# Short merge jobs of a hybrid attention block moved forward and spread by running sums

## The chip, the cores and the metric

The kernel runs on one core of one Trainium2 chip. The metric is the device time of one execution in microseconds (us). Five engines work side by side and meet only at semaphores: TensorE (PE), ScalarE (ACT), VectorE (DVE), GpSimd (POOL) and SyncE (SP), which here only issues transfers.

## What is computed

The input x has 256 tokens of 2048 channels. In short:

```
h  = RMSNorm(x);  z = h @ w_in            # q, k, v, gate of 16 heads, forget logits, two merge gates
oa = rmsnorm(diff_attention(...)) * silu(ga);   ya = oa @ w_proj_a      # 8 heads
ob = forgetting_attention(...)    * silu(gb);   yb = ob @ w_proj_b      # 8 heads
m  = sigmoid(ma) * ya + sigmoid(mb) * yb
out = RMSNorm(x + m @ w_out)
```

All is float32. Each product is made of three TensorE passes over operands split into a high and a low half (hi*hi, hi*lo, lo*hi).

## The kernel before

**Jobs.** The weights come in tiles of 128 x 1024 floats (512 KB). A job is one such tile. It is loaded by SyncE into one of four raw slots (`load`, L291 on); ScalarE makes its high half (`split`, L614), VectorE its low half (`split`, L845), each in a ring of four slots; TensorE multiplies it (`tile` and `sum_tile`, matmuls on L342 to L344). Job t + 4 may be split only when TensorE has done job t, since it takes the ring slot. All engines go through the jobs in one fixed order; in the iteration of job t ScalarE splits job t + 4, and VectorE splits job t + 4 and, where that job needs it, adds for job t + 5.

**Long jobs.** Chunk c (2 to 15) is the input projection of head c: eight long jobs of 12 matmuls, 512 columns each, into two PSUM banks (one for each half of the tokens). When the last is done, ScalarE empties both banks into `z_sb` (`evacuate`, L619); TensorE may write these banks again only after that (`banks_free`). The projections of the forgetting branch (FOX, 16 jobs), of the differential branch (DIFF, 16 jobs) and the output projection (OUT, 32 jobs) are long jobs too. The code numbers the chunks from 0; the jobs of chunk 2 begin at job 20.

**Short jobs.** The merge gates are computed by a Strassen-like scheme: for each of four groups seven products P1, P5, P6, P3, P7, P4, P2 in this order, each of four short jobs of 6 matmuls, 112 in all. They write bank Z2 or Z3 in turn. For P5, P6, P7 and P4 VectorE first combines the raw weights with an earlier tile (`add`, L858 and L860, 128 x 1024). P1 and P5 are copied out by ScalarE (`keep`), the others are added by VectorE (`fold`, L869 to L881: P6 and P7 take two additions of 128 x 512, the others one). The sums of activations that P5, P6, P3 and P7 need are split in four parts (ScalarE L682, VectorE L968) at the jobs in `PARTS_AT`.

**Order.** Each of the chunks 3 to 15 and the first half of FOX has 16 jobs, 8 long and 8 short, nearly alternating (`HEAD_STEPS`, `SUM_STEPS`); a chunk ends with a long job and two short ones, and begins with a long one. Chunk c's long jobs use banks Z0 and Z1 (chunk 2: Z2 and Z3). Chunks 2, DIFF, OUT and the second half of FOX hold long jobs alone.

**Attention.** The attention of head b is done beside the jobs, in two bursts on TensorE after a given job: X (`X_AT`: transposes of the gated output of b - 2, of the probabilities of b - 1, of q and k of b) and Y (`Y_AT`: values of b - 1, scores of b). Around them ScalarE does copies, exponentials and tanh, VectorE the low half of q and k (L986), the gate (L991), the gated output (L1021) and the masked maxima (L979, L981), GpSimd the bias of the next forgetting head (L1207, L1212) or the rotary embedding. `O_SPLIT_AT` places the splits of attention outputs.

The wait of a short job for its bank is, in `sum_tile`:

```python
fill = FORMS * g + f
if fill < 2:
    pe.wait_ge(evac[0], 4)      # chunk 2 evacuated
    pe.wait_ge(evac[1], 4)
else:
    form_taken(fill - 2)
```

Of the kernel before, what the change touches and what calls it, by code (L numbers as in the profile page):

```python
# [44 lines left out]
HEAD_STEPS, SUM_STEPS = (0, 2, 4, 6, 8, 10, 12, 13), (1, 3, 5, 7, 9, 11, 14, 15)  # L45
FOX_STEPS, FOX_SUM_STEPS = (0, 2, 4, 5, 8, 11, 14, 15), (1, 3, 6, 7, 9, 10, 12, 13)
SUM_JOB = ([MIXED_JOB + 16 * c + u for c in range(N_HEADS - 3) for u in SUM_STEPS] + [FOX_JOB + u for u in FOX_SUM_STEPS])
SUM_OF = {job: s for s, job in enumerate(SUM_JOB)}
X_AT = {21: 0, 28: 1, 38: 2, **{MIXED_JOB + 16 * (b - 2) + 4: b for b in range(3, N_HEADS)},
        FOX2_JOB + 1: N_HEADS, DIFF_JOB + 1: N_HEADS + 1}  # L50
Y_AT = {25: 0, 33: 1, 43: 2, **{MIXED_JOB + 16 * (b - 2) + 9: b for b in range(3, N_HEADS)}, FOX2_JOB + 5: N_HEADS}
# [10 lines left out]
def head_job(c, j):  # L62
    if c == 0:
        return j
    return PLAIN_JOB + j if c == 2 else MIXED_JOB + 16 * (c - 3) + HEAD_STEPS[j]


# [16 lines left out]
DIFF_OF = {diff_job(n, j): (n, j) for n in range(4) for j in range(4)}  # L84

# [18 lines left out]
def build(nc, x, xT, xg, consts_in, w_main, w_fl, g_final, out):  # L104
# [11 lines left out]
    with ctx:  # L116
# [6 lines left out]
        def sem(name):  # L123
# [89 lines left out]
        LAST = ((0, slice(3 * CHUNK, 4 * CHUNK), Z[0]),  # L213
                (1, slice(3 * CHUNK, 7 * CHUNK // 2), Z[1]), (1, slice(7 * CHUNK // 2, 4 * CHUNK), A))
# [125 lines left out]
        def _(pe):  # L340
# [197 lines left out]
            for job in range(MIXED_JOB, FOX_JOB):  # L538
                if job in HEAD_OF:
                    c, j = HEAD_OF[job]  # L540
                    if j == 0:
                        banks_free(4 if c == 3 else fill_of(c) + 1)
                    z_tile(c, j)
                else:
                    sum_tile(SUM_OF[job])
                attention(job)

            def fox_tile(n, j):
                if j == 0:
                    banks_free((18, 19, 19, 20)[n])  # L550
                    if n == 2:
                        form_taken(FORMS * GROUPS - 2)
                        form_taken(FORMS * GROUPS - 1)
                if n == 0:
                    pe.wait_ge(o_split, j // 2 + 1)
                tile(fox_job(n, j), 1 if n == 2 else 0, oT_hi, oT_lo, 2 * j, 2, CHUNK, j == 0, j == 3)

            for job in range(FOX_JOB, DIFF_JOB):
                if job in FOX_OF:
                    fox_tile(*FOX_OF[job])  # L560
                else:
                    sum_tile(SUM_OF[job])
# [40 lines left out]
        def _(act):  # L603
# [223 lines left out]
        def _(dve):  # L827
# [238 lines left out]
            def fox_gate(n):  # L1066
# [3 lines left out]
                for m in range(M_TILES):  # L1070
                    dve.scalar_tensor_tensor(m_all[:, n, m, :], gates[:, n, m, 1, :], 1.0, Z[(2 if n == 2 else 0) + m][:],
                                             ALU.add, ALU.mult).then_inc(evac[m], 1)

            def diff_gate(n):
# [5 lines left out]
                for m in range(M_TILES):  # L1080
                    dve.scalar_tensor_tensor(m_b[:, m, :], gates[:, n, m, 0, :], 1.0, Z[2 * (1 - n % 2) + m][:],
# [224 lines left out]
```

## Time and profile before

| | us |
|---|---|
| median of 3 runs (740.04 to 740.54) | 740.09 |
| the profiled execution | 740.02 |
| its span, first to last instruction | 738.2 |
| TensorE busy | 728.4 |
| VectorE busy | 560.0 |
| ScalarE busy | 438.3 |
| GpSimd busy | 84.2 |

An engine's busy time counts its instructions' durations; matmuls overlap, so starts tell more than durations. In a timeline a row has the start, the time taken (of the merged instructions), engine, line, operation, output and inputs, the count, and in brackets the idle time before it and what ended it. By the trace chunk 3 begins at 77.9 us, each mixed chunk takes about 35 us, FOX begins at 537.2 and DIFF at 595.6.

### The profile page before, as it was taken

To read this page: it belongs to the slowest core of one execution; us is meant where nothing else is said; L and a number is where in the kernel's file an instruction comes from. 1 tells how busy PE (TensorE), PEld (TensorE's weight loads), DVE (VectorE), ACT (ScalarE), POOL (GpSimd) and SP (SyncE) were. 2 spreads that over 40 slices of the span, in tenths; PEclk is the share of its full clock that TensorE was granted. 3 is DMA by queue.
4 is the path that set the end of the run, shared out by engine and by line. 5 is a ranking of instruction groups with operands and counts; after the bars stand their busy time and mean duration, and the time that the engine had idled before them with its cause. 6 is when DMAs were issued, how large, how long until landed. Compare 5 with 4: busy or idle time off the path is not lost.

```text
span 738.2 us, 9729 instructions
## 1 busy us (share of the span) xinstructions
PE 728.4 (99%) x3538; PEld 609.4 (83%) x3538; DVE 560.0 (76%) x724; ACT 438.3 (59%) x652; POOL 84.2 (11%) x105
## 2 busy tenths in 40 slices
PE   8999999999999999999999999999999999999996
PEld 6998888888888888888888888888888888888886
DVE  6775798779669778877978976988998657655552
ACT  7963667466656565666656667667567544444531
POOL 0000223103010201010302010202020000001110
PEclk9999999999999999999999999999999999999999
DMA  8668465776956676785586766566677656756632
GB/s 330 212 209 332 146 228 203 250 225 236 340 171 237 220 248 224 271 289 192 203 273 199 270 247 262 198 259 224 221 249 248 200 193 228 292 191 187 193 140 115
DMA packets 47230, 168.97 MB, mean 229 GB/s; under 512 B 5256, under 2 KB 5264, under 8 KB 46672
## 3 DMA queue, kind: packets, MB, share of 16 engines
q1 hardware_dynamic: 46064, 164.97, 64.6%
q10 hardware_dynamic: 864, 1.84, 0.7%
q0 software_dynamic: 256, 1.54, 0.5%
q8 instruction: 29, 0.48, 0.3%
q14 instruction: 17, 0.14, 0.1%
HBM read 166.23 MB, written 2.11 MB: 228 GB/s over the span
## 4 chain that ended last, share of the span: by engine, by line
PE 94%; DVE 2%; issue 2%; DMA 1%; ACT 1%; SPq 0%; DVEq 0%; POOLq 0%; POOL 0%; ACTq 0%
PE Z L342 29%; PE Z L343 28%; PE Z L344 28%; PE Z L503 3%; PE A L444 1%; DVE w_lo L845 1%; PE A L410 1%; DMA w_raw<-in_w_main 1%; PE B L426 1%; PE Dk L435 1%; PE B L423 1%; DVE gates L912 1%; PE C L453 0%; ACT w_hi L614 0%; PE A L461 0%
## 5 line engine op out<-in xcount | busy, mean ns | idle before, releaser
L845 DVE TENSOR_TENSOR w_lo<-w_raw,w_hi 128x1024 fp32r<-128x1024 f32 (+1 forms) x240 | 290.5, 1215 | 113.4 <-ACT w_hi L614 110.9
L614 ACT ACTIVATE w_hi<-w_raw 128x1024 fp32r<-128x1024 f32 (+1 forms) x235 | 243.7, 1044 | 184.5 <-PE Z L344 162.3
L342 PE MATMUL Z<-w_hi,hT_hi 128*128 128x512 f32 (+2 forms) x720 | 274.4, 381 | 0.5 <-DVE w_lo L845 0.5
L344 PE MATMUL Z<-w_hi,hT_lo 128*128 128x512 f32 (+2 forms) x720 | 272.7, 379 | 0.0
L343 PE MATMUL Z<-w_lo,hT_hi 128*128 128x512 f32 (+2 forms) x720 | 272.7, 379 | 0.0
L342 PEld LDWEIGHTS Z<-w_hi,hT_hi 128*128 128x128 f32 x720 | 135.3, 188 | 26.9 <-issue 0.6
L344 PEld LDWEIGHTS Z<-w_hi,hT_lo 128*128 128x128 f32 x720 | 135.3, 188 | 25.4
L343 PEld LDWEIGHTS Z<-w_lo,hT_hi 128*128 128x128 f32 x720 | 135.3, 188 | 24.5
L342 PE MATMUL Z<-w_hi,sum_hi 128*128 128x512 f32 x256 | 101.2, 395 | 0.0
L344 PE MATMUL Z<-w_hi,sum_lo 128*128 128x512 f32 x256 | 99.8, 390 | 0.0
L343 PE MATMUL Z<-w_lo,sum_hi 128*128 128x512 f32 x256 | 99.7, 390 | 0.0
L845 DVE TENSOR_TENSOR w_lo<-x_and_g,w_hi 128x1024 fp32r<-128x1024 f32 x64 | 80.3, 1255 | 25.1 <-ACT w_hi L614 24.2
L614 ACT ACTIVATE w_hi<-x_and_g 128x1024 fp32r<-128x1024 f32 x64 | 67.9, 1060 | 52.1 <-DVE x_and_g L860 32.6
L860 DVE TENSOR_TENSOR x_and_g<-w_raw,x_and_g 128x1024 f32<-128x1024 f32 x48 | 59.1, 1232 | 2.7 <-DMA w_raw<-in_w_main 2.7
L344 PEld LDWEIGHTS Z<-w_hi,sum_lo 128*128 128x128 f32 x256 | 48.1, 188 | 10.2
L342 PEld LDWEIGHTS Z<-w_hi,sum_hi 128*128 128x128 f32 x256 | 48.1, 188 | 9.7 <-issue 0.3
L343 PEld LDWEIGHTS Z<-w_lo,sum_hi 128*128 128x128 f32 x256 | 48.1, 188 | 9.5
L1207 POOL TENSOR_TENSOR bias<-gates,c_nat 128x128 f32<-128x128 f32 (+1 forms) x16 | 16.3, 1040 | 151.3 <-DVE neg_max L981 145.6
L619 ACT ACTIVATE z_sb<-Z,rstd 128x512 f32<-128x512 f32 x29 | 18.4, 686 | 20.9 <-PE Z L344 19.8
L1237 POOL TENSOR_TENSOR o_rstd<-o_ms,neg_half 128x2 f32<-128x2 f32 x8 | 9.2, 1156 | 188.1 <-DVE o_ms L1058 188.1
L1225 POOL TENSOR_TENSOR rope_t<-z_sb,consts 128x64 f32<-128x64 f32 x32 | 14.7, 492 | 111.1 <-ACT z_sb L619 111.1
L858 DVE TENSOR_TENSOR w_raw<-x_and_g,w_raw 128x1024 f32<-128x1024 f32 x16 | 19.7, 1229 | 5.0 <-DMA w_raw<-in_w_main 5.0
(184 smaller groups left out, 567.4 us busy)
## 6 DMA issues: line engine op xcount, KB each, us to landing
w_raw<-in_w_main SPq DMA_DIRECT2D x283, 512.0 KB, 4.1
x_and_g<-in_w_main SPq DMA_DIRECT2D x16, 512.0 KB, 7.1
w_raw<-in_w_fl SPq DMA_DIRECT2D x8, 264.0 KB, 3.0
o_T<-in_x SPq DMA_DIRECT2D x1, 2048.0 KB, 7.9
x_and_g<-in_xT SPq DMA_DIRECT2D x4, 256.0 KB, 5.9
gates<-c_rows_dram POOLq DMA_DIRECT2D x1, 1024.0 KB, 6.1
z_sb<-in_g_final SPq DMA_DIRECT2D x1, 1024.0 KB, 9.9
x_and_g<-in_xT ACTq DMA_DIRECT2D x3, 256.0 KB, 7.3
```

Of the source, the lines that this page charges most:

```text
L342: pe.matmul(acc, a_hi, b_hi, start=first, stop=False)
L343: pe.matmul(acc, a_hi, b_lo, start=False, stop=False)
L344: return pe.matmul(acc, a_lo, b_hi, start=False, stop=last)
L503: mm = pe.matmul(Z[m][:], x_part[:, 2 * j + kk, m * P:(m + 1) * P], w_part[:, kk], start=(j == 0 and part == 0 and kk == 0), stop=(j == TI ...
L614: act.activation(w_hi[:, t % RING, 0:cols_of(t)], weights(t), ACT.Copy).then_inc(hi_ready, 1)
L619: act.activation(z_sb[:, c % Z_SLOTS, m], Z[(2 if c == 2 else 0) + m][:], ACT.Copy, scale=rstd[:, m:m + 1]).then_inc(evac[m], 1)
L845: dve.tensor_tensor(w_lo[:, t % RING, 0:n], weights(t), w_hi[:, t % RING, 0:n].bitcast(fp32), ALU.subtract).then_inc(lo_ready, 1)
L858: dve.tensor_tensor(raw, chain[:, q, :], raw, ALU.subtract).then_inc(added, 1)
L860: dve.tensor_tensor(chain[:, q, :], raw, chain[:, q, :], ALU.subtract).then_inc(added, 1)
L1207: pool.tensor_tensor(bias[:, sl].unsqueeze(1), rows.rearrange("p (h n) -> p h n", h=HEADS)[:, h:h + 1, 0:n], c_nat[:, m, h:h + 1].unsqueez ...
L1225: ins = pool.tensor_tensor(rope_t[:, i], u, v, ALU.mult)
L1237: pool.tensor_tensor(o_rstd[:], o_ms[:], neg_half[:], ALU.pow).then_inc(o_rstd_ready, 1)
```

## The change

All 112 short jobs now stand in chunks 3 to 12, 7 to 16 in each (`SUMS_IN`). `ORDER` writes out each chunk as a string of `h` (long) and `s` (short). Chunks 13, 14, 15 and FOX have long jobs only. Bursts and splits get new places. Long jobs of a chunk without short ones, and everything behind, take the two pairs of banks in turn (`PAIR`). Chunk 3 now begins with three short jobs, at job 28. The total count of jobs, DIFF and OUT stay as they are.

```diff
-HEAD_STEPS, SUM_STEPS = (0, 2, 4, 6, 8, 10, 12, 13), (1, 3, 5, 7, 9, 11, 14, 15)
-FOX_STEPS, FOX_SUM_STEPS = (0, 2, 4, 5, 8, 11, 14, 15), (1, 3, 6, 7, 9, 10, 12, 13)
+SUMS_IN = {3: 11, 4: 11, 5: 15, 6: 10, 7: 16, 8: 10, 9: 9, 10: 13, 11: 10, 12: 7, 13: 0, 14: 0, 15: 0, 2: 0}
+ORDER = {3: 'ssshssshshshshshshh', 4: 'ssshssshshshhshshsh', 5: 'shhssshssshssshssshshsh', 6: 'shshhssshssshshshh', 7: 'shshshshssshssshssshsssh', 8: 'shshshshhssshsshsh', 9: 'shshhshshshshsssh', 10: 'ssshssshssshshshshshh', 11: 'ssshsshshshshhshsh', 12: 'shshhssshsshhhh', 13: 'hhhhhhhh', 14: 'hhhhhhhh', 15: 'hhhhhhhh', 2: 'hhhhhhhh'}
+CHUNK_JOB = [0, 0, PLAIN_JOB]
+for c in range(3, N_HEADS + 1):
+    CHUNK_JOB.append(CHUNK_JOB[-1] + len(ORDER[c - 1]))
+BURST_X = {3: 8, 4: 8, 5: 3, 6: 4, 7: 4, 8: 4, 9: 4, 10: 8, 11: 7, 12: 4, 13: 2, 14: 2, 15: 2}
+BURST_Y = {3: 13, 4: 12, 5: 14, 6: 12, 7: 11, 8: 8, 9: 8, 10: 15, 11: 12, 12: 11, 13: 6, 14: 6, 15: 6}
-O_SPLIT_AT = {FOX_JOB - 20: 0, FOX_JOB - 14: 1, FOX2_JOB + 3: 2, FOX2_JOB + 4: 3}
+O_SPLIT_AT = {CHUNK_JOB[14] + 1: 0, CHUNK_JOB[14] + 4: 1, CHUNK_JOB[15] + 4: 2, FOX_JOB + 7: 3}
+PAIR = [0, 1, 0, 1]
+for c in range(3, N_HEADS):
+    PAIR.append(0 if SUMS_IN[c] else 1 - PAIR[-1])
+for n in range(11):
+    PAIR.append(1 - PAIR[-1])
-            def banks_free(fill):
-                pe.wait_ge(evac[0], fill - 1)
-                pe.wait_ge(evac[1], fill - 1)
+            def banks_free(fill, pair):
+                before = [n for n in range(fill) if PAIR[n] == pair]
+                if before:
+                    pe.wait_ge(evac[0], before[-1] + 1)
+                    pe.wait_ge(evac[1], before[-1] + 1)
```

The first jobs of the chunks are 28 (chunk 3), 47, 66, 89, 107, 131, 149, 166, 187, 205 (chunk 12), 220, 228 and 236 (chunk 15); FOX begins at 244 and DIFF, as before, at 260. In the new order P1 takes jobs 28, 29, 30, 32, P5 33, 34, 36, 38, P6 40, 42, 44, 47, P3 48, 49, 51, 52 and P7 53, 55, 57, 60. The first X bursts follow jobs 21, 28, 40 and 55, the Y bursts jobs 25, 32, 45 and 59.

## Rows read from the trace of the kernel before

**Rows 1.** The page: busy time of the engines; granted clock in 40 slices

```profile
PE 728.4 (99%) x3538; PEld 609.4 (83%) x3538; DVE 560.0 (76%) x724; ACT 438.3 (59%) x652; POOL 84.2 (11%) x105
...
PEclk9999999999999999999999999999999999999999
```

**Rows 2.** Timeline of PE: first matmul of job 28; around short job 58

```profile
77.90 0.39 PE L342 MATMUL Z<-w_hi,hT_hi 128*128 128x512 f32 x1
...
146.86 0.39 PE L344 MATMUL Z<-w_hi,hT_lo 128*128 128x512 f32 x1
...
148.45 0.39 PE L342 MATMUL Z<-w_hi,sum_hi 128*128 128x512 f32 x1
```

**Rows 3.** Timelines of DVE and PE around the one gap

```profile
296.56 1.21 DVE L845 TENSOR_TENSOR w_lo<-w_raw,w_hi 128x1024 fp32r<-128x1024 f32 x1
...
297.45 0.39 PE L344 MATMUL Z<-w_hi,hT_lo 128*128 128x512 f32 x1
297.92 0.47 PE L342 MATMUL Z<-w_hi,hT_hi 128*128 128x512 f32 x1
```

**Rows 4.** Groups of DVE by line and shape: busy us, mean ns

```profile
L845 DVE TENSOR_TENSOR w_lo<-w_raw,w_hi 128x1024 fp32r<-128x1024 f32 x232 | 284.9, 1233 | 109.9 <-ACT w_hi L614 107.4 <-ACT w_hi L814 1.8
...
L986 DVE TENSOR_TENSOR qkT_lo<-A,qkT_hi 128x384 fp32r<-128x384 f32 x16 | 8.8, 552 | 0.7 <-ACT qkT_hi L688 0.7
...
L991 DVE SCALAR_TENSOR_TENSOR gate<-gate_tanh,z_sb 128x256 f32<-128x256 f32 x16 | 6.7, 419 | 0.0
...
L869 DVE TENSOR_TENSOR gates<-Z,gates 128x512 f32<-128x512 f32 x4 | 2.7, 682 | 0.0
```

**Rows 5.** Timeline of DVE: a Y burst's work, adds, low halves

```profile
118.38 0.60 DVE L1021 SCALAR_TENSOR_TENSOR og<-A,inv,gate 128x128 f32<-128x128 f32 x2
...
119.45 1.22 DVE L860 TENSOR_TENSOR x_and_g<-w_raw,x_and_g 128x1024 f32<-128x1024 f32 x1
120.59 1.42 DVE L845 TENSOR_TENSOR w_lo<-w_raw,w_hi 128x1024 fp32r<-128x1024 f32 x1
121.94 1.63 DVE L845 TENSOR_TENSOR w_lo<-x_and_g,w_hi 128x1024 fp32r<-128x1024 f32 x1
...
123.56 1.41 DVE L860 TENSOR_TENSOR x_and_g<-w_raw,x_and_g 128x1024 f32<-128x1024 f32 x1
```

**Rows 6.** Timeline of ACT: the evacuations of chunks 2 and 4

```profile
78.10 1.27 ACT L619 ACTIVATE z_sb<-Z,rstd 128x512 f32<-128x512 f32 x2
79.26 1.06 ACT L614 ACTIVATE w_hi<-x_and_g 128x1024 fp32r<-128x1024 f32 x1
80.20 1.06 ACT L682 ACTIVATE sum_hi<-gates 128x1024 fp32r<-128x1024 f32 x1
...
147.29 1.27 ACT L619 ACTIVATE z_sb<-Z,rstd 128x512 f32<-128x512 f32 x2 [1.66 <-PE Z L344]
```

**Rows 7.** Waits of DVE from 77.9 to 537.2: total, times, longest

```profile
DVE w_lo L845 <- ACT w_hi L614: 68.8, 75, 2.6
DVE w_raw L858 <- DMA w_raw<-in_w_main: 5.0, 7, 2.1
```

**Rows 8.** Timeline of PE: before and after an X burst, a Y burst

```profile
80.39 0.40 PE L344 MATMUL Z<-w_hi,hT_lo 128*128 128x512 f32 x1
...
81.31 0.48 PE L342 MATMUL Z<-w_hi,hT_hi 128*128 128x512 f32 x1
...
171.03 0.39 PE L344 MATMUL Z<-w_hi,hT_lo 128*128 128x512 f32 x1
...
172.50 0.39 PE L342 MATMUL Z<-w_hi,hT_hi 128*128 128x512 f32 x1
```

**Rows 9.** Timeline of POOL: the bias of one head

```profile
119.61 2.87 POOL L1207 TENSOR_TENSOR bias<-gates,c_nat 128x128 f32<-128x128 f32 x2 [19.46 <-DVE neg_max L981]
122.56 2.73 POOL L1212 TENSOR_TENSOR bias<-bias,consts 128x128 f32<-128x128 f32 x2
```

**Rows 10.** Transfers by tile: count, KB each, median us to landing

```profile
w_raw<-in_w_main SPq DMA_DIRECT2D x283, 512.0 KB, 4.1
```

More of the change, by code:

```diff
@@ L59, in fill_of, with max_count @@
     return c if c < 2 else c + 1
+def max_count(heads):
+    return 2 * heads + 2 * max(0, heads - HEADS)
 def head_job(c, j):
@@ L64, in head_job @@
         return j
-    return PLAIN_JOB + j if c == 2 else MIXED_JOB + 16 * (c - 3) + HEAD_STEPS[j]
-def max_count(heads):
-    return 2 * heads + 2 * max(0, heads - HEADS)
+    return CHUNK_JOB[c] + [u for u, kind in enumerate(ORDER[c]) if kind == "h"][j]
 def fox_job(n, j):
-    return FOX_JOB + FOX_STEPS[4 * n + j] if n < 2 else FOX2_JOB + 4 * (n - 2) + j
+    return FOX_JOB + 4 * n + j
 def diff_job(n, j):
@@ L355, in tile @@
                 mm.then_inc(w_used, 1)
-            def banks_free(fill):
-                pe.wait_ge(evac[0], fill - 1)
-                pe.wait_ge(evac[1], fill - 1)
+            def banks_free(fill, pair):
[3 more added lines that the diff above has]
+                    pe.wait_ge(evac[1], before[-1] + 1)
+                if pair == 1 and fill > FIRST_SUM_FILL:
+                    form_taken(FORMS * GROUPS - 2)
+                    form_taken(FORMS * GROUPS - 1)
             def z_tile(c, j):
-                tile(head_job(c, j), 1 if c == 2 else 0, hT_hi, hT_lo, 2 * j, 2, CHUNK, j == 0, j == TILES - 1)
+                tile(head_job(c, j), PAIR[fill_of(c)], hT_hi, hT_lo, 2 * j, 2, CHUNK, j == 0, j == TILES - 1)
             def form_taken(fill):
@@ L549, in fox_tile @@
                 if j == 0:
[L550 to L553, printed above, removed]
+                    banks_free(FOX_FILL + n, PAIR[FOX_FILL + n])
                 if n == 0:
                     pe.wait_ge(o_split, j // 2 + 1)
-                tile(fox_job(n, j), 1 if n == 2 else 0, oT_hi, oT_lo, 2 * j, 2, CHUNK, j == 0, j == 3)
+                tile(fox_job(n, j), PAIR[FOX_FILL + n], oT_hi, oT_lo, 2 * j, 2, CHUNK, j == 0, j == 3)
             for job in range(FOX_JOB, DIFF_JOB):
[L559 to L562, printed above, removed]
+                fox_tile(*FOX_OF[job])
                 attention(job)
             for n in range(4):
-                banks_free(21 + n)
+                banks_free(DIFF_FILL + n, PAIR[DIFF_FILL + n])
                 for j in range(4):
@@ L576, in _ @@
             for n in range(3):
-                banks_free(25 + n)
+                banks_free(OUT_FILL + n, PAIR[OUT_FILL + n])
                 for j in range(TILES):
@@ L618, in evacuate @@
                 for m in range(M_TILES if c >= 2 else 1):
-                    act.activation(z_sb[:, c % Z_SLOTS, m], Z[(2 if c == 2 else 0) + m][:], ACT.Copy,
+                    act.activation(z_sb[:, c % Z_SLOTS, m], Z[2 * PAIR[fill_of(c)] + m][:], ACT.Copy,
                                    scale=rstd[:, m:m + 1]).then_inc(evac[m], 1)
@@ L1126, in residual @@
                 sl = slice(n * CHUNK, (n + 1) * CHUNK)
-                dve.tensor_tensor(y_sb[:, m, sl], Z[2 * (1 - n % 2) + m][:], x_res[:, m, sl], ALU.add).then_inc(evac[m], 1)
+                dve.tensor_tensor(y_sb[:, m, sl], Z[2 * PAIR[OUT_FILL + n] + m][:], x_res[:, m, sl], ALU.add).then_inc(evac[m], 1)
             for n in range(3):
```

36 lines of the change are left out of this document (19 added, 17 removed).

## The prediction

> **What bounds the kernel now.** I read the page's busy shares first, then who waited for whom, then TensorE's timeline. TensorE is busy 728.4 of 738.2 us at the full granted clock [rows 1]. Busy alone says little for a pipelined engine, so I went by starts: the last matmul of long job 57 starts at 146.86, and the six of short job 58 and one more later it is 148.45 [rows 2]: 1.59 / 7 = 0.227 us from start to start of 512-column matmuls. A long job (12 matmuls) is 2.72 us, a short one (6) is 1.36 us. From chunk 3 on TensorE stands still behind a low half once: VectorE ends at 297.77, TensorE starts at 297.92, where 297.68 was due, so 0.25 us is lost and 0.14 us passes from an end to the start that it releases [rows 3]. TensorE's own work is the bound, VectorE is just fast enough, and nothing but those 0.25 us is there to be won in the stages that the change touches.
>
> **The change, part by part.** It removes no matmul, add, fold or transfer. It moves 112 short jobs from thirteen chunks and the FOX stage into chunks 3 to 12, and leaves chunks 13 to 15 and FOX with long jobs alone.
>
> *VectorE's prices.* A low half lasts 1.23 us, an add the same [rows 4, 5], and starts follow each other at 1.14 us [rows 5], as ops overlap by 0.09; a high half on ScalarE takes 1.06 and its starts are 0.95 apart [rows 6]. A short job with an add thus asks 2.28 us of VectorE for 1.36 us of TensorE; a long job asks 1.14 for 2.72. The low half of job t+4 can't begin before TensorE is through job t, for its ring slot and the high half. So VectorE leads by three jobs at most: 6.8 us with alternating jobs, 4.1 to 5.4 where short jobs stand together. On average VectorE would do (it waits 68.8 us for ScalarE in 77.9 to 537.2 [rows 7]), but slack before a clump can't be stored beyond three jobs. I walked the clumps.
>
> *(a) Job 28, the first after chunk 2.* Before it is a long job in banks Z0 and Z1, so TensorE goes on at 77.90 while ScalarE empties Z2 and Z3 from 78.10 to 79.37 [rows 2, 6]. Now job 28 is a short job that writes Z2, and its first matmul waits for both evacuations: 79.37 + 0.14 - 77.90 = **1.6 us**. Behind it every later matmul is late; nothing covers it.
>
> *(b) Six chunk boundaries.* At the starts of chunks 5 to 9 and 12 (by the code's numbers) only one short job stands between the last long job of the chunk before and the first of the new one, in the same banks. Take the evacuation of chunk 4: its last long matmul starts at 146.86, a short job would end at 148.45, ScalarE's two evacuations end at 147.29 + 1.27 = 148.56 [rows 2, 6], plus 0.14: 0.25 us. Six times 1.5; at two of the six (8 and 12) ScalarE first waits for an add ahead of the evacuation, at an estimated 0.4 each. **2.3 us.** Before, two short jobs stand there and hide it.
>
> *(c) Chunk 3, jobs 28 to 37.* Time from the end of job 27. TensorE: job 28 ends at 1.6 + 1.36 = 3.0; then the X burst 0.69 and the Y burst 1.24 [rows 8], short jobs 29, 30, 32, 33, 34, 36 (8.2) and long 31, 35 (5.4): job 37 is due at 18.5. VectorE: ScalarE evacuates first, so the high half of 31 ends at 2.4; low half 31, sum_lo part, add 33 bring VectorE to 5.8. Then low halves 32 to 37, adds 34, 36, 38 and a sum_lo part, 10 x 1.14 = 11.4, and the head's own work: qkT_lo 0.55 and gate 0.42, less the overlaps 0.8 [rows 4], og and maxima 1.07, from 118.38 to 119.45 [rows 5]: 19.1, usable at 19.3. Late by 0.8. While GpSimd adds a head's bias, VectorE's ops last 1.42, 1.63 and 1.41 us in place of 1.23, 0.8 us in all [rows 5, 9]; with it 1.6. I take **1.3 us**.
>
> *(d) Chunk 4, jobs 47 to 54.* Time from the end of long job 46. TensorE: 47, 48, 49 short, 50 long: 51 is due at 6.8. ScalarE evacuates (0.2 to 1.35), makes high half 50 (to 2.4), sum_hi (to 3.4), high half 51 (to 4.3). VectorE: low half 50 to 3.6, sum_lo to 4.75, the two chained adds of the P6 fold (0.68 each [rows 4]) to 6.2, low half 51 to 7.4: ready 7.57, late 0.76. Add 53 and low half 52 follow: ready 9.85 where 8.93 was due, late 0.92. Then low half 53, add 55, low half 54: ready 13.34 where 12.57 was due, late 0.77. **2.45 us.** Before, long jobs alternate there.
>
> *(e) The other clumps* (jobs 76 to 86, 95 to 101, 123 to 130, 171 to 179, 188 to 193) have a similar mix, but no evacuation, sum split and fold together at their start. Three marginal delays of 0.3: **0.9 us**, an estimate between 0 and 3. The bounds come from (c) and (d): none if VectorE enters with a full lead, one more chunk 4 if not.
>
> *(f) Transfers.* A raw load takes 4.1 us from issue to landing [rows 10] and VectorE already waits seven times, 5.0 us, for loads of P7 [rows 7]. In a clump a slot's next load has three jobs of VectorE, 3 x 2.28 = 6.8 us, to land, so I cost it at nothing. Where VectorE catches up through P3 or P2 jobs the cover is only three short jobs, 4.1 us; losing it costs under 1 us a place, 2 to 3 us in all.
>
> *(g) Chunks 13 to 15 and FOX.* Long jobs alone, VectorE leads by up to three long jobs; banks alternate, so evacuations are covered by a whole chunk. Probabilities of a head are combined three jobs after its Y burst, and the next X burst comes at the fourth: some 2 us of cover. Nothing gained, as TensorE lost nothing there before; nothing lost. If the cover is gone, a few tenths four times. The O splits move within chunks in which both engines idle: nothing. The pair chosen for the out stage only swaps banks.
>
> Minus the 0.25 us of now: 1.6 + 2.3 + 1.3 + 2.45 + 0.9 - 0.25 = **+8.3 us**. The profiled execution took 740.02 us (span 738.2), the median is 740.09; both give 748.3.
>
> **A rule weighed against the trace.** While GpSimd works, VectorE's ops stretched to between 1.41 and 1.63 us [rows 5], not to the length of GpSimd's two pairs of 2.87 and 2.73 us [rows 9]. The Trainium skill (SBUF — State Buffer, "Who interferes with whom") says that a VectorE op with two SBUF inputs and a GpSimd op that reads SBUF exclude each other, and that the later one blocks for the other's whole instruction. By that rule the sum would go up as in rival 3; the rows here show a smaller price.
>
> **The rivals.**
> 1. *Low halves keep up; only banks wait.* The planner's running sum may place shorts where VectorE has its idle time, and my walks chain durations without slack. Then (a) and the six plain waits stay: 1.6 + 1.5 - 0.25, **742.9**. For it: 68.8 us of slack [rows 7]. Against: 2.28 against 1.36 us. Chance 0.17.
> 2. *More clumps late, and loads with them.* (e) at its upper end (+2) and (f) at 3: **753**. For it: loads are waited for even now. Chance 0.14.
> 3. *GpSimd's bias blocks VectorE fully* in the clumps: 5.6 us of GpSimd per head [rows 9] less the 0.8 counted would cost up to 4.8 more in each of (c) and (d), of which I count 3 each: **754.3**. Against: rows 5. Chance 0.05.
> 4. *Not slower.* ScalarE's evacuation is wholly behind the single short job, every low half is in time and the gap of rows 3 goes: 740.1 + 1.6 - 0.25 = **741.4**, inside what can't be told from no change. It decides at job 51: if its low half is ready 6.8 us after job 46, this case or rival 1 holds. If job 28's wait too were partly hidden, the time would be just under before. Chance 0.08. That the change doesn't do what it says I see no way for: the order is written out.
>
> **How the numbers follow.** My forecast (746 to 751.5) has 0.56. The range 742.5 to 753.5 leaves out rivals 3 and 4 and half of what lies at rival 2's upper end, about 0.2. About 0.2%, 1.5 us, is what a measurement of this kernel can tell from no change. Slower by more than that: the forecast and rivals 1 to 3, 0.92; within: most of rival 4, 0.05; faster: its rest, 0.03.
>
> **What would show it.** TensorE should idle about 1.6 us before job 28, released by ScalarE's z_sb; about 0.25 us at six chunk starts, released the same way; and 0.7 to 1 us three times between jobs 51 and 54, released by VectorE's low half. VectorE's waits for ScalarE should move from chunks 3 to 12 to chunks 13 to FOX. TensorE's 0.227 us should not move. The prediction is wrong if the low halves of 51 to 54 are in time, if the bursts of chunks 13 to 15 wait, or if waits behind loads are a main item.

## The result, and the profile after

The changed kernel is slower: median 754.91 us of 6 executions (751.96 to 756.27) against 740.07 us (739.71 to 740.54) before; ratio 1.0193, 95% interval 1.0177 to 1.0208. That is +14.8 us where +8.3 was forecast, and above the range. Two things stand out. The profiled execution is the fastest of the six (751.96 us, span 750.1), and the executions lie 4.3 us apart, where those of before lie within 0.8. So 11.9 us can be read in the trace, and 3 us more are in what differs from one execution to the next; that part has to be argued from other kernels' traces.

The page of the changed kernel: busy time, granted clock, and the groups of VectorE's adds.

```profile
PE 732.7 (98%) x3538; PEld 607.7 (81%) x3538; DVE 562.6 (75%) x724; ACT 438.8 (58%) x652; POOL 72.3 (10%) x105
...
PEclk9999999999999999999999999999999999999998
...
L873 DVE TENSOR_TENSOR x_and_g<-w_raw,x_and_g 128x1024 f32<-128x1024 f32 x48 | 59.7, 1243 | 4.5 <-DMA w_raw<-in_w_main 4.1
...
L871 DVE TENSOR_TENSOR w_raw<-x_and_g,w_raw 128x1024 f32<-128x1024 f32 x16 | 19.6, 1226 | 5.4 <-DMA w_raw<-in_w_main 5.4
```

The work is the same ([rows 1, 4]): 3538 matmuls, 64 adds of 1.23 to 1.24 us. In this execution the clock stays full. The page's busy shares hide what happened; the starts of TensorE show it. Around job 28, TensorE, then ScalarE, then GpSimd:

```profile
77.77 0.39 PE L358 MATMUL Z<-w_hi,hT_lo 128*128 128x512 f32 x1
80.13 0.47 PE L356 MATMUL Z<-w_hi,hT_hi 128*128 128x512 f32 x1 [1.97 <-ACT z_sb L632]
...
77.86 0.40 ACT L718 ACTIVATE probs<-probs,neg_max 128x128 f32<-128x128 f32 x1 [1.32 <-DVE neg_max L994]
...
78.75 1.24 ACT L632 ACTIVATE z_sb<-Z,rstd 128x512 f32<-128x512 f32 x2
...
75.10 0.97 POOL L1220 TENSOR_TENSOR bias<-gates,c_nat 128x128 f32<-128x128 f32 x2 [6.11 <-DMA gates<-c_rows_dram]
```

TensorE loses 80.13 - 77.77 - 0.23 = 2.13 us. Its last matmul of job 27 ends at 77.77 + 0.39 = 78.16, but ScalarE starts to evacuate only at 78.75: until then it was at head 0's exponentials, behind the maxima, behind GpSimd's bias, behind a load that took 6.1 us to be waited out. Chunk 4, the clump that I walked, in TensorE's and VectorE's timelines:

```profile
129.27 0.39 PE L358 MATMUL Z<-w_hi,hT_lo 128*128 128x512 f32 x1
130.24 0.47 PE L356 MATMUL Z<-w_hi,sum_hi 128*128 128x512 f32 x1 [0.58 <-DVE w_lo L858]
...
131.47 0.40 PE L358 MATMUL Z<-w_hi,sum_lo 128*128 128x512 f32 x1
132.57 0.47 PE L356 MATMUL Z<-w_hi,sum_hi 128*128 128x512 f32 x1 [0.71 <-ACT w_hi L627]
...
135.17 0.39 PE L358 MATMUL Z<-w_hi,sum_lo 128*128 128x512 f32 x1
136.12 0.47 PE L356 MATMUL Z<-w_hi,hT_hi 128*128 128x512 f32 x1 [0.56 <-ACT w_hi L627]
...
125.14 1.23 DVE L858 TENSOR_TENSOR w_lo<-w_raw,w_hi 128x1024 fp32r<-128x1024 f32 x1 [2.84 <-ACT w_hi L627]
126.28 1.22 DVE L981 TENSOR_TENSOR sum_lo<-gates,sum_hi 128x1024 fp32r<-128x1024 f32 x1
127.42 0.69 DVE L882 TENSOR_TENSOR gates<-Z,gates 128x512 f32<-128x512 f32 x1
128.14 0.69 DVE L884 TENSOR_TENSOR gates<-gates 128x512 f32<-128x512 f32 x1
128.87 1.23 DVE L858 TENSOR_TENSOR w_lo<-w_raw,w_hi 128x1024 fp32r<-128x1024 f32 x1
```

Each interval between two starts less 0.227 is a loss: 0.74 before job 51, 0.88 before 52, 0.72 before 54. VectorE's queue is the one walked: low half 50, sum part, two additions of the P6 fold, low half 51. The same subtraction for every job start of chunks 3 to 12 gives this account of the profiled execution (us):

| where | forecast | measured |
|---|---|---|
| job 28, chunk 2's banks | 1.6 | 2.13 |
| chunk 3, jobs 35, 37, 39 | 1.3 | 1.04 |
| chunk 4, jobs 51, 52, 54 | 2.45 | 2.34 |
| six boundaries, jobs 67, 90, 108, 132, 150, 206 | 2.3 | 3.37 |
| other low halves (101, 130, 148, 179, 193) | 0.9 | 1.14 |
| sum of waits | 8.55 | 10.02 |
| restart of TensorE behind each of the 18 waits | - | 2.0 |
| the gap of [rows 3] | -0.25 | -0.25 |
| sum | 8.3 | 11.8 |

The restart is a term that I did not have. A short job without a wait ahead of it takes 1.13 us from its first to its last start, job 51 takes 131.47 - 130.24 = 1.23; long jobs take 2.61 for 2.50. The first interval after a wait is 0.31 in place of 0.23. 0.11 us by 18 waits is 2.0, and 740.02 + 11.8 = 751.8 meets the 751.96 measured. The bursts cost the same as before: 34.4 us in all in both traces, from chunk 3 to the end of FOX. Chunks 13 to 15 and FOX run as forecast: an X burst puts 0.90 us between two jobs there and a Y burst 1.54, as in the kernel before, and nothing waits. VectorE's waits for ScalarE moved as forecast too: 39.2 us in chunks 3 to 12, where the kernel before has 53.5, and 36.8 from chunk 13 to the end of FOX.

### The profile page after: what moved, and what is told of

Read it like the earlier page. It is cut to its first block, busy times and chain, and to the rows that moved or that the text cites. A ratio compares the mean times of both kernels' runs of the same rounds, so it can differ in the third digit from the quotient of the medians.

```text
span 750.1 us, 9736 instructions
## 1 busy us (share of the span) xinstructions
PE 732.7 (98%) x3538; PEld 607.7 (81%) x3538; DVE 562.6 (75%) x724; ACT 438.8 (58%) x652; POOL 72.3 (10%) x105
## 3 DMA queue, kind: packets, MB, share of 16 engines
q0 software_dynamic: 256, 1.54, 0.5%
## 4 chain that ended last, share of the span: by engine, by line
PE 81%; DVE 8%; DMA 4%; issue 3%; ACT 2%; POOL 0%; SPq 0%; DVEq 0%; POOLq 0%; ACTq 0%
PE Z L356 25%; PE Z L358 24%; PE Z L357 24%; DVE w_lo L858 4%; DMA w_raw<-in_w_main 3%; PE Z L522 3%; ACT w_hi L627 2%; PE A L463 1%; DVE w_raw L871 1%; DVE x_and_g L873 1%; DMA gates<-c_rows_dram 1%; PE A L429 1%; DMA c_rows_dram<-c_neg 1%; PE Dk L454 1%; PE B L445 1%
## 5 line engine op out<-in xcount | busy, mean ns | idle before, releaser
L356 PEld LDWEIGHTS Z<-w_hi,sum_hi 128*128 128x128 f32 x256 | 48.1, 188 | 11.9 <-issue 1.3
L1220 POOL TENSOR_TENSOR bias<-gates,c_nat 128x128 f32<-128x128 f32 (+1 forms) x16 | 14.4, 923 | 179.9 <-DVE neg_max L994 173.8
L1250 POOL TENSOR_TENSOR o_rstd<-o_ms,neg_half 128x2 f32<-128x2 f32 x8 | 7.4, 930 | 176.4 <-DVE o_ms L1071 176.4
L1238 POOL TENSOR_TENSOR rope_t<-z_sb,consts 128x64 f32<-128x64 f32 x32 | 9.3, 324 | 117.7 <-ACT z_sb L632 117.7
```

The source lines that it names most:

```text
L356: pe.matmul(acc, a_hi, b_hi, start=first, stop=False)
L1220: pool.tensor_tensor(bias[:, sl].unsqueeze(1), rows.rearrange("p (h n) -> p h n", h=HEADS)[:, h:h + 1, 0:n], c_nat[:, m, h:h + 1].unsqueez ...
L1238: ins = pool.tensor_tensor(rope_t[:, i], u, v, ALU.mult)
```

## The experiments

Names with b_ start from the kernel before, those with a_ from the changed one. Ratios are to the kernel before, run on the same chip.

**1. b_short_first: the first wait alone.**

```diff
 def head_job(c, j):
+    if c == 3 and j == 0:
+        return MIXED_JOB + 1
...
+SUM_JOB[0] = MIXED_JOB
```

> The kernel before, with jobs 28 and 29 exchanged: chunk 3 begins with a short job, nothing else moves. Theory 1 (only TensorE's waits count): the short job waits for both evacuations, 1.6 to 2.1 us and about 0.1 for the restart, so 740.1 + 1.7 to 2.2 = 741.8 to 742.3 in every execution, granted clock 0.998 throughout. Theory 2 (the wait's length hangs on a chain at the start of attention - forget rows through memory, bias, maxima, exponentials - which differs between executions, and where it is long TensorE's granted clock falls to 1.2 GHz for a while): a spread of some 4 us, 742 to 746, with a mean granted clock near 0.993 in the slow ones. Rival: the wait is paid back later, because VectorE gains lead meanwhile: 740.1 to 740.5.

Median 746.46 us (744.90 to 748.75), ratio 1.0088 (1.0066 to 1.0109): an exchange of two jobs costs 6.5 us, three quarters of what I had forecast for the whole change. Theory 2 holds, more strongly than I put it. TensorE, ScalarE and GpSimd in its trace, then the window behind the wait (length; busy TensorE, weight loads, VectorE, ScalarE, GpSimd; granted clock, DMA share, GB/s):

```profile
77.45 0.39 PE L347 MATMUL Z<-w_hi,hT_lo 128*128 128x512 f32 x1
82.37 0.77 PE L345 MATMUL Z<-w_hi,hT_hi 128*128 128x512 f32 x1 [4.54 <-ACT z_sb L622]
82.93 0.63 PE L346 MATMUL Z<-w_lo,hT_hi 128*128 128x512 f32 x1
83.36 0.63 PE L347 MATMUL Z<-w_hi,hT_lo 128*128 128x512 f32 x1
...
80.09 0.40 ACT L708 ACTIVATE probs<-probs,neg_max 128x128 f32<-128x128 f32 x1 [3.88 <-DVE neg_max L984]
...
80.98 1.24 ACT L622 ACTIVATE z_sb<-Z,rstd 128x512 f32<-128x512 f32 x2
...
77.36 0.96 POOL L1210 TENSOR_TENSOR bias<-gates,c_nat 128x128 f32<-128x128 f32 x2 [8.87 <-DMA gates<-c_rows_dram]
78.41 0.87 POOL L1215 TENSOR_TENSOR bias<-bias,consts 128x128 f32<-128x128 f32 x2
```

```profile
82.30:87.00 4.70, 4.63 (x15) 3.94 (x16) 3.04 (x4) 3.45 (x5) 0.68 (x2) 0.52 0.30 111
```

The load of the forget rows was waited for 8.87 us here, against 6.11 in the trace of the changed kernel. The wait at job 28 is 4.70 us, and behind it matmuls start 0.43 us apart: the granted clock is at its lower level of 1.2 GHz (0.52 in this window) up to 86.8 us. The Trainium skill (TensorE: Matmul & The Clock Gate, "HAM oscillation — how this bites in real kernels") describes a matmul stream that throttles each time it has waited for a transfer. The trace agrees, with a wait for ScalarE that goes back to a transfer: 4.70 us of wait, then 0.52 of the clock. Job 28's five intervals take 2.27 us in place of 1.13, and the X burst behind them 0.86 us more than before: about the 1.9 us that this execution took beyond 740.0 + 4.7.

Six traces have a short job at 28, the whole load of the rows and head 0's exponentials ahead of the evacuation. The longer the wait for the load, the longer the wait at job 28, but for 0.1 us between the last three (us):

| trace | wait for the load | wait at job 28 |
|---|---|---|
| changed kernel | 6.11 | 2.13 |
| experiment 7 | 7.57 | 3.26 |
| experiment 8 | 7.91 | 4.07 |
| experiment 3 | 8.60 | 4.77 |
| experiment 4 | 8.73 | 4.66 |
| experiment 1 | 8.87 | 4.70 |

How late the load can be in the kernel before at no cost is an estimate from its rows: its first short job starts at 81.31 [rows 8], and the evacuation that it needs is usable at 79.37 + 0.14, so 1.8 us. Whether this load varies as much there is not shown, since there is one trace of that kernel (5.66 us).

**2. a_long_first: a long job in front of chunk 3.**

```diff
-ORDER = {3: 'ssshssshshshshshshh', ...}
+ORDER = {3: 'hssshssshshshshshsh', ...}
```

> The kernel after, with chunk 3's order changed from ssshsssh... to hssshsssh...: the last long job is taken out and put in front, so job 28 writes Z0 and Z1 and waits for nothing. Theory 1: the 2.1 us wait and its restart go, median 754.9 - 2.2 = 752.7, and the spread of 4 us stays, having another cause. Theory 2: the spread goes with the wait: all executions at 752.0 - 2.2 = 749.8, within 0.5 us, mean granted clock 0.997 to 0.998. Rival: the clump behind comes earlier and takes the gain back: 752 or more.

Median 752.71 us (750.69 to 753.47), ratio 1.0165 (1.0148 to 1.0183), clock 0.997 or more in all. The two theories are both half right: no half clock any more, but 2.8 us of spread stay, so there is a second source. The rival holds as well: in the trace the low halves of chunk 3 (jobs 32, 35, 36, 38) lose 0.36 + 0.49 + 1.14 + 0.93 = 2.92 us where the changed kernel lost 1.04, so most of the 2.1 us of the first wait came back behind it. And the long job in front does not hide everything. Here the rows' load was waited for 7.05 us, and the first short job, 29, still waits for the bank behind the X burst, which with this wait takes 1.11 us in place of 0.69:

```profile
80.19 0.39 PE L358 MATMUL Z<-w_hi,hT_lo 128*128 128x512 f32 x1
...
81.53 0.47 PE L356 MATMUL Z<-w_hi,hT_hi 128*128 128x512 f32 x1 [0.18 <-ACT z_sb L632]
```

**3. a_two_shorts: two short jobs at the six boundaries.**

```diff
-5: 'shhssshssshssshssshshsh'
+5: 'sshhsshssshssshssshshsh'   # likewise 6 to 9 and 12
...
```

> The kernel after, with two short jobs instead of one at the head of chunks 5 to 9 and 12 (the next short job of the chunk is moved to the front). Theory 1: the six bank waits (0.21, 0.33, 0.21, 0.49, 0.92, 1.21, together 3.37 us) and six restarts of 0.1 go: 3.5 to 4 us less, median about 751, the best execution about 748.2; the spread between executions stays. Rival: the waits at chunks 9 and 12 are VectorE's lateness under another name, and come back as waits for a low half: only 1.3 us less.

Median 751.55 us (750.66 to 753.71), ratio 1.0158 (1.0139 to 1.0178): 3.4 less than the changed kernel. No wait for a bank is left at the six boundaries, but job 206, now a short job, waits 0.80 us for its low half, and waits for low halves elsewhere rise from 1.14 to 2.68 (0.93 at job 101, 0.45 at 65, 0.41 at 177). The profiled execution had the long kind of first wait, 4.77 us, and behind it no wait in chunk 3. Both the theory and its rival are in it: some boundary waits were VectorE's lateness seen through ScalarE.

**4. a_thin_adds: adds of 32 columns.** It leaves out 31/32 of each combination of weights.

```diff
-dve.tensor_tensor(chain[:, q, :], raw, chain[:, q, :], ALU.subtract)
+dve.tensor_tensor(chain[:, q, 0:32], raw[:, 0:32], chain[:, q, 0:32], ALU.subtract)   # likewise for P7
```

> The kernel after, with the 64 adds of combined weights cut from 1024 to 32 columns (it leaves out 31/32 of each combination of weights): 1.1 us less of VectorE per add, all semaphores as they are. Theory 1: VectorE is late only because of the adds; all waits for low halves from job 33 on (4.5 us) and their restarts (about 1.3), and the excess over 0.25 us at chunks 8, 9 and 12 (1.9 us), go: 7 to 8 us less, median 747 to 748, best 744 to 745. Rival: loads or ScalarE's high halves set the low halves' time: 2 us less at most.

Median 747.77 us (745.87 to 749.51), ratio 1.0094 (1.0077 to 1.0112): 7.1 less than the changed kernel, as the theory had it. All six boundary waits are 0.21 us, the plain price of an evacuation behind one short job (forecast 0.25). Of the waits for low halves only 0.74 and 0.30 in chunk 4 are left, where the sum split and the fold stand. So without adds VectorE has time, and the excess at the boundaries (3.37 - 6 x 0.21 = 2.1 us) was VectorE's. Chunk 3's waits are no evidence here: they are gone too in experiments 3 and 7, whose adds are whole and whose first wait was long (4.77 and 3.26 us) like the 4.66 us here. VectorE still waits 15.7 us for loads in this trace (9.5 in the changed kernel's), so a late load costs TensorE something only where VectorE has no time to spare.

**5. b_short_rows: the load of the rows cut, head 0 first.**

```diff
-pool.dma_start(rows, c_rows_dram... [P, HEADS * SEQ])).then_inc(rows_loaded, 16)
+pool.dma_start(rows[:, 0:SEQ], c_line[:, 0:SEQ]...).then_inc(rows_loaded, 16)
 pool.wait_ge(rows_loaded, 16)
+pool.dma_start(rows[:, SEQ:], c_line[:, SEQ:]...).then_inc(rows_loaded, 16)   # waited for at head 1
```

> The kernel before with jobs 28 and 29 exchanged, and the load of the forget rows cut in two: the 256 columns of head 0 come first (1 KB a partition in place of 8), the other heads' rows after. With the load whole this exchange cost 4.8 to 8.7 us, and its trace shows a wait of 4.7 us and 6.8 us of granted half clock. Theory (the length of the wait hangs on the load of the rows, through bias, maxima and exponentials that ScalarE does ahead of the evacuation): head 0's rows land 3 us or more earlier, the exponentials are done when job 27 ends, and only the two evacuations are left: wait 1.6 to 1.7 us, no half clock, 741.8 to 742.2 in every execution. Rival (the store of the rows or another part of the chain varies): spread stays at 2 us or more, some executions above 744.

Median 744.01 us (742.06 to 744.54), ratio 1.0045 (1.0032 to 1.0059): 2.5 less than with the load whole, but not the 741.8 to 742.2 expected. An eighth of the data is not an eighth of the time: GpSimd still waited 5.81 us for head 0's rows in this trace, and job 28 2.5. The edit has a cost of its own: GpSimd issues the second load, 0.53 us, between the first one's landing and the bias. The lower median bears the chain out, the size does not; experiment 9 takes the chain away by order instead.

**6. a_rows_split: the same cut in the changed kernel.**

> The kernel after with the load of the forget rows cut in two, head 0's 256 columns first. Theory: job 28's wait is 1.6 to 1.7 us in every execution, no half clock behind it; median 751.3 to 751.8 against 754.9, all executions within 1 us. Rival: the spread has a second source in the clumps, where loads land sooner or later: spread 2 us or more at a median of 752 to 753.

Median 752.05 us (750.91 to 753.09), ratio 1.0158 (1.0144 to 1.0172). Head 0's rows came after 4.17 us, job 28 waited 1.61 us, the forecast's value, and the clock stayed full. The spread of 2.2 us is the rival's: job 206 lost 1.66 us here and 1.21 in the changed kernel's trace.

**7. a_parts_early: the last sum split four jobs earlier.**

```diff
-PARTS_AT = {..., MIXED_JOB + 18: 3}
+PARTS_AT = {..., MIXED_JOB + 14: 3}
```

> The kernel after, with the last of the four splits of the activation sums (1.05 us of ScalarE, 1.22 of VectorE) in the iteration of job 42 in place of 46. Theory (chunk 4's three waits, 0.74 + 0.88 + 0.72, come from evacuation, sum split and P6 fold standing together ahead of the clump): in my walk job 51 is in time, job 52 late by 0.35, job 54 by 0.7: 1.05 in place of 2.34 us and one restart of 0.1 less, so 1.4 us less than the kernel after in a like execution; median about 753.5, and the three gaps are to be read in the trace. Rival (the adds alone are too much for jobs 51 to 54): the three gaps stay within 0.3 us in all.

Median 753.02 us (752.77 to 754.29), ratio 1.0175 (1.0161 to 1.0189). The interval overlaps that of the changed kernel, so the waits decide, not the median. Job 51 is in time, 52 late by 0.58, 54 by 0.71: 1.29 in place of 2.34 us, where the walk gave 1.05. This execution also shows the second source of the spread. Chunk 12's first long job, and the load ahead of it, in this trace:

```profile
451.85 0.39 PE L358 MATMUL Z<-w_hi,hT_lo 128*128 128x512 f32 x1
454.80 0.47 PE L356 MATMUL Z<-w_hi,hT_hi 128*128 128x512 f32 x1 [2.57 <-DVE w_lo L858]
...
436.12 1.22 DVE L871 TENSOR_TENSOR w_raw<-x_and_g,w_raw 128x1024 f32<-128x1024 f32 x1 [2.13 <-DMA w_raw<-in_w_main]
...
452.49 1.06 ACT L627 ACTIVATE w_hi<-x_and_g 128x1024 fp32r<-128x1024 f32 x1 [2.73 <-DVE x_and_g L873]
453.45 1.25 ACT L632 ACTIVATE z_sb<-Z,rstd 128x512 f32<-128x512 f32 x2
```

and the same places in the changed kernel's:

```profile
452.55 0.39 PE L358 MATMUL Z<-w_hi,hT_lo 128*128 128x512 f32 x1
453.99 0.47 PE L356 MATMUL Z<-w_hi,hT_hi 128*128 128x512 f32 x1 [1.05 <-DVE w_lo L858]
...
435.30 1.23 DVE L871 TENSOR_TENSOR w_raw<-x_and_g,w_raw 128x1024 f32<-128x1024 f32 x1 [0.74 <-DMA w_raw<-in_w_main]
```

VectorE waits 1.39 us longer for one load of P7, and 16 us later TensorE loses 2.73 us in place of 1.21. The load itself was slow: in both traces VectorE wanted it 3.6 us after its issue, and it landed after 4.3 us in the changed kernel's and after 5.7 in this one. In between VectorE's rows follow each other without a wait in both traces, and ScalarE's high half, then its evacuation, stand behind VectorE's add. The bracket at 454.80 names a low half, but the evacuation is what ends just before, at 453.45 + 1.25 = 454.70.

**8. a_even: the same counts, spread evenly.**

```diff
-5: 'shhssshssshssshssshshsh', 12: 'shshhssshsshhhh'
+5: 'sshsshshsshshsshsshshss', 12: 'sshshhshhshshhs'   # likewise 3 to 11
...
```

> The kernel after with the same number of short jobs in each chunk, but spread evenly: two shorts at a chunk's head, then one or two after each long job, nowhere three in a row but at two chunk ends. Theory (what counts is the run of shorts with adds against a lead of three jobs, not the load of a chunk): the bank waits of the six boundaries go (3.4 us), and waits for low halves fall from 4.5 us to 1 or 2: 6 to 7 us less with restarts; median 748 to 749, the best near 745.5; job 28's wait and its spread stay. Rival (VectorE is short of time over whole chunks, with 10 to 16 shorts in each): the waits for low halves stay at 4 us or more and the median at 751 or more.

Median 762.75 us (760.15 to 763.78), ratio 1.0299 (1.0276 to 1.0322): a miss of my theory, the worst kernel of all. It holds three things. First, I had put a short job at the very end of chunk 12:

```profile
489.30 0.39 PE L358 MATMUL Z<-w_hi,hT_lo 128*128 128x512 f32 x1
494.31 0.77 PE L356 MATMUL Z<-w_hi,hT_hi 128*128 128x512 f32 x1 [4.62 <-DVE gates L894]
```

Chunk 13 writes the banks of the short jobs, and waits until VectorE has folded P2, behind two heads' worth of attention work: 4.8 us, and the clock at half up to 499.3. Second, without this and the wait at job 28 (4.1 us) the trace still has 8.2 us of waits in chunks 4 to 12, against 6.9 in the same chunks of the changed kernel. Third, the order is not the even one that I announced. A chunk ends with one or two short jobs and the next begins with two, so at all nine boundaries from chunk 4 to chunk 12 three or four short jobs stand together: 46 to 48, 65 to 67, 87 to 90, 106 to 108, 129 to 132, 148 to 150, 165 to 167, 186 to 188, 204 to 206. All of the 8.2 us stand in six of these runs or within three jobs behind one: jobs 51, 65, 66, 68, 89, 91, 111, 133 and 205 to 207. So the experiment does not tell whether even spacing helps. The median of 751 or more and the waits of 4 us or more fit the rival, that VectorE is short over whole chunks, but a run of short jobs against a lead of three jobs explains them as well. An order with no such run was not tried.

**9. b_short_evac: exponentials behind the evacuation.**

```diff
-if job - 1 in Y_AT and Y_AT[job - 1] < N_HEADS:
+if job - 1 in Y_AT and 0 < Y_AT[job - 1] < N_HEADS:
     exps(Y_AT[job - 1])
+if job - 2 in Y_AT and Y_AT[job - 2] == 0:
+    exps(0)
```

> The kernel before with jobs 28 and 29 exchanged, and head 0's exponentials on ScalarE put behind chunk 2's evacuation (one iteration later). Theory (the evacuation was late because ScalarE stood, in order, at exponentials that wait for the maxima, these for the bias, this for the loaded rows): the first wait is 1.6 us whatever the load takes; the X burst behind job 28 then waits about 0.8 us for the probabilities, since the exponentials come after the high half of job 31; no half clock in any execution. 740.1 + 1.6 + 0.8 + 0.1 to 0.2 = 742.6 to 742.8, executions within 1 us. Rival (the maxima keep VectorE so long that job 30 or 31 waits for its low half instead): the same 2 to 5 us in total at another place, spread as before.

Median 743.07 us (742.93 to 744.08), ratio 1.0040 (1.0026 to 1.0054). Four of five executions lie within 0.15 us. TensorE and GpSimd:

```profile
77.39 0.39 PE L347 MATMUL Z<-w_hi,hT_lo 128*128 128x512 f32 x1
79.23 0.47 PE L345 MATMUL Z<-w_hi,hT_hi 128*128 128x512 f32 x1 [1.45 <-ACT z_sb L622]
...
80.46 0.40 PE L347 MATMUL Z<-w_hi,hT_lo 128*128 128x512 f32 x1
81.90 0.55 PE L438 MATMUL Dk<-consts,probs 128*128 128x128 f32 x3 [1.04 <-ACT probs L710]
...
77.13 0.96 POOL L1212 TENSOR_TENSOR bias<-gates,c_nat 128x128 f32<-128x128 f32 x2 [8.88 <-DMA gates<-c_rows_dram]
```

The load is as late as in experiment 1 (8.88 and 8.87 us), and yet the first wait is 1.61 us and the clock stays full. The X burst waits 1.3 us (1.95 us between jobs 28 and 29 in place of 0.69), 0.5 more than expected. With the load late and the harm gone, the cause is the order on ScalarE, not the load alone.

**10. a_evac_ahead: the same in the changed kernel.**

> The kernel after with head 0's exponentials put behind chunk 2's evacuation. Theory: job 28 waits 1.6 us, the X burst 0.8, no half clock: like the best executions of the kernel after or a little over, 751.9 to 753, median 752.5 against 754.9. The rest of the spread (750.9 to 753.1 with the rows' load cut) comes from VectorE's queue ahead of chunk 12 and stays, 1 to 2 us. Rival: median 754 or more, the wait only moving to low halves in chunk 3.

Median 753.68 us (751.94 to 755.32), ratio 1.0180 (1.0163 to 1.0197). Job 28 waits 1.61 us, the burst behind it 1.3, the clock is full (0.996 or more); but the median is 1.2 above the expected, and the spread is 3.4 us. Chunk 3's low halves now lose 1.54 us and job 206 1.82. The median is only 1.2 below the changed kernel's, and the intervals of the two ratios overlap: a gain is not shown, though the first wait is cured.

**11. a_combined: four repairs together** (2, 3, 7 and 9).

> The kernel after with all four repairs: long job first in chunk 3, two shorts at the head of chunks 5 to 9 and 12, the last sum split at job 42, exponentials behind the evacuation. Theory (waits add up, TensorE's own work is the floor at 740): from 752.0 of the profiled execution job 28's 2.2 go, of the six bank waits and their sequels about 1.8 net, chunk 4's 1.2: 746.8; median 747 to 748, never below 741, so no better than the kernel before. Rival (VectorE short of time over whole chunks, so that each repair only moves its lateness on): 750 or more.

Median 747.64 us (747.16 to 748.49), ratio 1.0100 (1.0087 to 1.0114), inside the expected 747 to 748. Its waits are the X burst's 1.6, chunk 4's 1.5 and some ten of 0.03 to 0.94 us. It beats the changed kernel by 7.3 us and not the kernel before: no order of the jobs makes TensorE's own work less.

**12. a_evac_thin: short jobs' loads cut to a quarter** (but for P1's), on top of 10. It leaves out three quarters of those raw weights; all engines' work stays whole.

```diff
+n = 256 if job in SUM_OF else cols_of(job)
-sp.dma_start(raw_slot(job), source(job))
+sp.dma_start(raw_slot(job)[:, 0:n], source(job)[:, 0:n])
```

> The kernel after with the exponentials behind the evacuation (753.7, from 751.9 to 755.3), and the loads of the short jobs' raw weights, but for P1's, cut to 256 of 1024 columns (it leaves out three quarters of those weights; VectorE's and ScalarE's work stays whole). Theory (what still varies is when loads land: in chunk 11 VectorE waited 0.74 us for a load of P7 in one trace and 2.13 in another, and the wait at job 206 was 1.21 and 2.73): VectorE's waits for loads, about 9.5 us in all, fall to 1 or 2; job 206 waits 0.2 to 0.8; the waits of chunk 4 (0.74, 0.87, 0.73) stay, as they need no load; median 751 to 752, executions within 1 us. Rival (loads are late only where VectorE would be late anyway): same median and spread as with whole loads.

Median 749.22 us (749.12 to 749.42), ratio 1.0116 (1.0099 to 1.0133): 4.5 us less than experiment 10, more than expected, and a spread of 0.3 us. VectorE's waits, this kernel's two longest, then the changed kernel's:

```profile
DVE w_lo L861 <- ACT w_hi L628: 147.8, 123, 3.1
DVE gates L1169 <- PE Z L359: 5.0, 2, 2.8
```

```profile
DVE w_lo L858 <- ACT w_hi L627: 139.7, 115, 3.1
DVE w_raw L871 <- DMA w_raw<-in_w_main: 5.4, 6, 1.6
...
DVE x_and_g L873 <- DMA w_raw<-in_w_main: 4.1, 8, 1.3
```

Of the adds' waits for loads, 9.5 us in 14, one of 0.5 us is left. So are chunk 3's waits, and job 206 loses 0.71, 150 0.21 us. Chunk 4's stay to 0.02 us (0.74, 0.89, 0.70), as do 101, 130 and 193 (0.24, 0.21, 0.44).

## Why the prediction was wrong

The direction was right, and TensorE waits at the places that were named. Two steps failed as mechanisms: the evacuation's time taken as fixed in (a), and the loads costed at nothing in (f). One term, the restart, was missing. The prediction named waits behind loads as a main item among the signs of being wrong, and they are one. In the profiled execution the 3.5 us over the forecast are the restart (2.0), (b) (1.1), (a) (0.5) and (e) (0.2), less 0.4 in (c) and (d); what the late loads cost stands within (b), (c) and (e). The median's other 3 us go with the long form of (a). By its own steps:

- *(a) job 28:* 1.6 us is right for the evacuations alone (1.61 in experiments 6, 9, 10, 12). The step that failed is to take the evacuation's time of 78.10 to 79.37 [rows 6] over into the new order as if only TensorE set it. In that trace it did, but by a hair: TensorE's last matmul of job 27 ends at 77.67 + 0.39 = 78.06, and ScalarE had left the exponentials at 77.97.

```profile
77.67 0.39 PE L344 MATMUL Z<-w_hi,hT_lo 128*128 128x512 f32 x1
...
77.79 0.18 ACT L707 ACTIVATION_READ_ACCUMULATOR probs<-probs,neg_max 128x1 f32 x1
```

  In front of them stands the chain that begins with a load, and there it could be some 1.9 us late at no cost (an estimate: the 0.1 us here and the 1.8 of experiment 1). In the new order every 0.1 us beyond the first is paid. **By its bare price the term is 1.6; as an exchange of two jobs it measured 6.5 at the median**, with 4.7 us of wait and half clock in the trace.
- *(b) boundaries:* the plain wait is 0.21, not 0.25. I had 0.4 extra at chunks 8 and 12 and none at 9; the trace has 0.28 at 8, 0.71 at 9, 1.00 at 12 and 0.12 at 6. The mechanism that I named, ScalarE waiting for an add, is the one in the rows of experiment 7; its size hangs on how late VectorE is.
- *(c)* came out at 1.04 for 1.3, but for another reason: the waits are 1.54 us in experiment 10 and vanish with thin loads in experiment 12, so they need late loads. My walk had none.
- *(d)* stands: 0.76, 0.92, 0.77 forecast, 0.74, 0.88, 0.72 measured, and in all six traces that keep this chunk's order, adds and sum split the same to 0.03 us, loads thin or whole. Moving the sum split removed 1.05 of 2.34 us.
- *(e)* 0.9 forecast, 1.14 measured in the trace, 0.89 with thin loads.
- *(f) transfers, "I cost it at nothing":* this is the main error besides (a). Thin loads took 4.5 us off. The step that failed is the cover of 6.8 us. In the changed kernel's trace the time from the issue of an add's load to the moment at which VectorE is ready for it is below 6.8 us at 46 of the 64 adds and below 4.1 at 18, down to 2.3, and these loads take 3.1 to 9.1 us to land. VectorE's waits for loads are 9.5 us, 7.7 before (5.0 for P7's [rows 7], 2.7 for the others'), so they hardly grew; but before, TensorE lost 0.25 us in all behind late low halves, and now more. An estimate, from what thin loads left in experiment 12: chunk 3's waits, those at 148 and 179 and part of those at 150 and 206, 2.5 us, with some 0.5 of restarts. That is the price which (f) itself names for lost cover, "2 to 3 us in all", and leaves out of the sum.
- *(g)* stands.
- *Missing:* the restart, 0.11 us behind each wait, 2.0 us in all. The trace of the kernel before shows it already: job 128, behind the gap of [rows 3], takes 2.60 us from first to last start for 2.50.

Of the rivals, the second (more clumps late, and loads with them, 753) came nearest by its cause, at a chance of 0.14: its 3 us for loads are there, its 2 us for other clumps are not. The third is nearest by its number, 754.3, and that is chance: chunk 4's waits came out at the length of a walk without any GpSimd term, and chunk 3's vanish with thin loads. Its price was also misread. The 2.87 and 2.73 us of [rows 9] are not GpSimd's own work: in experiment 1's trace, where VectorE is idle, the same two pairs take 0.96 and 0.87 us. So beside VectorE GpSimd's instructions were stretched as well, VectorE's 0.8 us (1.0 with a fourth instruction of 1.48 us at 124.90) stands against 1.8 and not against 5.6, and these rows do not tell against the rule that the prediction weighed. With thin loads, and without the 1.3 us that experiment 10's order adds at the X burst, the changed kernel would be near 748 (749.2 - 1.3, an estimate), and the sum of (a) to (e) gives 748.3. That this agrees is partly luck: with loads in time (c) is nothing in place of 1.3, and the restarts that were left out, 0.11 at each of 13 waits, are 1.4.

The median's 3 us over the profiled execution are not read from a trace of that very kernel. Four of its six executions have a mean clock of 0.993 to 0.995 where the other two have 0.997 and 0.998: (0.998 - 0.993) x 2 x 750 = 7.5 us at the lower level. The traces of experiments 1, 3, 4, 5, 7 and 8 show 3.4 to 6.8 us of it behind job 28, those of 2, 6, 9, 10, 11 and 12 none. What the long form costs can be read by comparing two traces that have the same code up to there: job 51 starts at 133.52 in experiment 3's, with a first wait of 4.77 us, and at 130.24 in the changed kernel's, with 2.13.

```profile
133.52 0.47 PE L356 MATMUL Z<-w_hi,sum_hi 128*128 128x512 f32 x1 [0.58 <-DVE w_lo L858]
```

These 3.3 us would take 751.96 to 755.2, where the four slower executions have 753.86 to 756.27. So the long form of this one wait fits them in time and in clock, though no trace shows it in the changed kernel itself; how the rest divides between the rows' load and the raw loads stays open, and so does what makes these loads land later in one execution than in another.

## What to carry to other kernels

An order of work that is balanced in its sums can still be late everywhere: what counts is how far one engine may lead (here three jobs of the ring), and which variable latency that lead was paying for. Before a wait is put behind a step that was done in time until now, follow that step's own queue back to the first load, and take the latest landing, not the median. Before an order is called even, write it out across the chunk boundaries. A wait costs more than its length: 0.1 us of restart each time, and half clock behind the long ones.

## What the runs showed of the hardware

- GpSimd's pairs of 128x128 additions took 0.96 and 0.87 us with VectorE idle, and 2.87 and 2.73 beside VectorE's 128x1024 ones, which lasted 1.41 to 1.63 us there in place of 1.23.
- TensorE's first interval between 512-column matmuls after a wait is 0.31 us for 0.227; a job behind a wait takes 0.11 us longer.
- After waits of 4.7 to 4.8 us, matmuls started 0.43 us apart, the granted clock being at 1.2 GHz for 6.8 us, part of it within the wait; with waits of 2.5, 3.3 and 4.1 us it was there for 3.4 us; behind waits of 1.6 to 2.1 us it stayed at 2.4 GHz. Over 77 to 92 us the granted clock was 0.77 in the three traces with waits of 4.7 to 4.8 us, and 0.89 in the three with 2.5 to 4.1 us.
- A GpSimd-issued broadcast of the forget rows to 128 partitions was waited for 5.7 to 8.9 us in the eleven traces that load it and the raw weights whole; an eighth of it still 4.2 and 5.8.
- Loads of 512 KB for the adds took 3.1 to 9.1 us from issue to landing in one trace. One that took 1.4 us longer than in another trace cost 1.5 us at the end, 16 us after it, when VectorE had no wait in between.
